# A two-model transformer step on one core: chosen mask ends the routing chain, second affine step beside the next index queries, residual factor inside the affine steps, MLP norm factor applied at the MLP's end

## The reference, cut to what matters

```
# first kind, l = 0, 1                                    ALPHA = 4 ** 0.25
mix = token_mixers(x, ...)               # differential and sparse attention, gates, w_out
x   = layer_norm(ALPHA * x + mix, ln1_g, ln1_b)
ffn = hierarchical_moe(x, ...)           # top group of 4, top 2 of its 8 experts, per token
ple = sigmoid(x @ w_ple_gate) * (p @ w_ple)
x   = layer_norm(ALPHA * x + ffn + ple, ln2_g, ln2_b)
# second kind, l = 0, 1
x = x + hybrid_mixer(rms_norm(x, attn_norm), ...)   # three attentions, gates, w_out
h = rms_norm(x, mlp_norm)
x = x + square(relu(h @ w_mlp_up)) @ w_mlp_down
# at the end
out = rms_norm(x, final_norm)
```

## Time and profile before

| what | value |
|---|---|
| three runs | 2030.92, 2035.6, 2040.48 us; median 2035.6 |
| the profiled execution | 2033.11 us, its span 2031.3 us |
| PE busy | 1913.3 us (94%) |
| DVE busy | 1414.3 us (70%) |
| ACT busy | 1076.6 us (53%) |
| POOL busy | 88.5 us (4%) |
| chain that ended last | 78% PE, 13% DVE, 4% ACT, 2% DMA, 1% POOL |

### The profile page before, as it was taken

One profiled execution on the slowest core, in us unless ns is written; L12 is line 12 of the kernel. 1 busy time (PEld: TensorE's weight loads), 2 busy tenths in 40 slices (PEclk: granted clock), 3 DMA queues, 4 the chain that ended last, 5 costly groups with the idle time before them and its releaser, 6 DMA issues.

```text
span 2031.3 us, 31158 instructions
## 1 busy us (share of the span) xinstructions
PE 1913.3 (94%) x12576; PEld 1750.0 (86%) x12576; DVE 1414.3 (70%) x2295; ACT 1076.6 (53%) x1686; POOL 88.5 (4%) x87
## 2 busy tenths in 40 slices
PE   7889989999889999999997899999998999999997
PEld 6779879999778898799896889998997889998997
DVE  5876778888668767898886666675445666675444
ACT  5454557777444545676773544444444645344443
POOL 2000010000010000100000000001001000001001
PEclk9999989999889999999998999999999999999999
DMA  7426169999444262799993343354554442454552
GB/s 288 145 84 235 48 261 408 389 408 420 167 166 146 104 229 71 296 414 374 422 421 121 130 154 137 125 187 148 190 191 170 157 160 105 146 184 148 187 189 82
DMA packets 60762, 426.77 MB, mean 210 GB/s; under 512 B 6928, under 2 KB 7056, under 8 KB 11584
## 3 DMA queue, kind: packets, MB, share of 16 engines
q1 hardware_dynamic: 59616, 421.65, 54.8%
q0 software_dynamic: 416, 1.81, 0.2%
q10 hardware_dynamic: 576, 1.19, 0.2%
HBM read 423.58 MB, written 1.05 MB: 209 GB/s over the span
## 4 chain that ended last, share of the span: by engine, by line
PE 78%; DVE 13%; ACT 4%; DMA 2%; issue 1%; POOL 1%; DVEq 0%; SPq 0%; ACTq 0%; POOLq 0%
PE bank L1041 63%; PE scp L1041 10%; DVE WSl L1384 4%; ACT WSh L1927 1%; PE bank L1135 1%; PE bank L1258 1%; ACT SC L1976 1%; DMA PT<-wts 1%; DMA ring<-wts 1%; PE bank L1120 1%; POOL sm L2163 1%; PE bank L1162 1%; DVE sm L1528 1%; DMA A<-wts 1%; PE bank L1278 1%
## 5 line engine op out<-in xcount | busy, mean ns | idle before, releaser
L1384 DVE TENSOR_TENSOR WSl<-ring,WSh 128x1024 fp32r<-128x1024 f32 (+3 forms) x512 | 591.2, 1198 | 213.9 <-ACT WSh L1927 212.2
L1927 ACT CAST WSh<-ring 128x1024 fp32r<-128x1024 f32 (+3 forms) x512 | 498.4, 1026 | 200.7 <-PE bank L1041 103.9
L1041 PE MATMUL bank<-XTh,WSh 128*128 128x256 f32 x1216 | 350.4, 288 | 7.2 <-DVE A L1563 4.4
L1041 PE MATMUL bank<-XTl,WSh 128*128 128x256 f32 x1216 | 346.6, 285 | 0.0
L1041 PE MATMUL bank<-XTh,WSl 128*128 128x256 f32 x1216 | 346.3, 285 | 0.0
L1041 PE MATMUL bank<-WSh,FA 128*128 128x512 f32 (+1 forms) x848 | 303.5, 391 | 3.9 <-DVE FA L1824 2.3
L1041 PE MATMUL bank<-WSl,FA 128*128 128x512 f32 (+1 forms) x680 | 264.0, 388 | 0.0
L1041 PEld LDWEIGHTS bank<-XTh,WSh 128*128 128x128 f32 x1216 | 236.1, 194 | 9.3 <-issue 5.5
L1041 PEld LDWEIGHTS bank<-XTl,WSh 128*128 128x128 f32 x1216 | 236.1, 194 | 0.2
L1041 PEld LDWEIGHTS bank<-XTh,WSl 128*128 128x128 f32 x1216 | 235.8, 194 | 0.0
L1041 PE MATMUL bank<-WSh,XTh 128*128 128x512 f32 (+4 forms) x544 | 205.3, 377 | 18.1 <-DVE WSl L1384 15.0
(11 more groups left out here) (279 smaller groups left out, 2939.4 us busy)
## 6 DMA issues: line engine op xcount, KB each, us to landing
ring<-wts SPq DMA_DIRECT2D x264, 1024.0 KB, 4.9
V<-wts SPq DMA_DIRECT2D x40, 1024.0 KB, 12.7
PT<-wts SPq DMA_DIRECT2D x30, 1024.0 KB, 9.7
H<-wts SPq DMA_DIRECT2D x28, 1024.0 KB, 9.3
GT<-wts SPq DMA_DIRECT2D x12, 1024.0 KB, 13.6
A<-wts SPq DMA_DIRECT2D x8, 1024.0 KB, 7.3
ring<-wts SPq DMA_DIRECT2D x8, 584.0 KB, 7.0
ring<-wts SPq DMA_DIRECT2D x4, 832.0 KB, 8.0
```

What stands on the lines that cost most here:

```text
L1041: return nc.tensor.matmul(dst, lhsT, rhs, start=start, stop=stop)
L1384: nc.vector.tensor_tensor(lo[:, c], buf[:, c], hi[:, c].bitcast(F32), ALU.subtract).then_inc(*lo_done.inc(("block", i)))
L1927: nc.scalar.copy(hi[:, c], buffers[s.buffer][:, c]).then_inc(*hi_done.inc(("half", i, k)))
```

## The change

1. `chosen` (MK) becomes a step of its own at the end of the routing chain, and the `lead` values become 14, 16 and 99, so that the chain ends ahead of the split that follows.
2. PE's spreading of the gains becomes the step `spread`, and DVE's part `affine` goes tile by tile. For `ln2` of the first layer, the two tiles stand after the index queries' steps of the second layer (`first_layer`, `if l:`).
3. ALPHA moves into the affine step: both instructions become scalar_tensor_tensor with the factor. POOL's multiplications go, except `scale_x` at `l == 0`.
4. `ROUTE_LATE` and `kept` stand after the eighth gather, not after the fourth.
5. In the second kind, `w_out`'s rows are transposed from X itself, the first half ahead of the last `w_out` block. `normed` "mlp" is gone. `factor` takes 1 / (mean square + eps), and `add_y` multiplies the MLP's result by it.
6. At the end, tile 0's statistics stand ahead of tile 1's sums, the final gain's row is spread into two banks ahead of the last block, and one instruction per half tile writes the output, which goes out in halves.
7. The pair of bn_stats after each `w_out` half stands behind both sums, in all four layers.
8. `pace` around the "ST" transposes is set otherwise; `spare` is empty there, and no instruction moves.

```diff
+    def affine(self, name, l, halves=range(T)):
+        for t in halves:
+            self.add("affine", name=name, l=l, t=t, scp=self.now("scp"))
...
                 f()
+            if l:
+                self.affine("ln2", l - 1, (c,))
...
-        self.add("scale_x", l=l)
+        if l == 0:
+            self.add("scale_x", l=l)
...
-        for c, self.lead in enumerate((0, 0, 12, 18, 18, 0)):
+        for c, self.lead in enumerate((0, 0, 14, 16, 99, 0)):
...
                 self.spare.extend(("route", dict(l=l, t=t, n=n)) for n in ROUTE_ORDER for t in range(T))
+                self.spare.append(("chosen", dict(l=l)))
...
-            if k == 3:
+            if k == KD - 1:
                 for n in ROUTE_LATE:
...
-        self.add("normed", name="mlp", l=l, n=D)
+        blocks = [f for c in range(2) for f in self.wide("w_out_2", "w_out", DEPTH + l, c, 512 * c, 512, ("merged", 2, l),
+                                                         owner="dve", row=l, fa=fa)]
         xt = self.use("XT", "pe")
-        self.turn_split("mlp", l, KD, xt=xt)
+        for f in blocks[0:3]:
+            f()
+        self.turn_split("mlp", l, 4, xt=xt)
+        blocks[3]()
+        self.turn_split("mlp", l, 4, at=2, xt=xt)
+        self.add("factor", l=l)
...
+                if l == DEPTH - 1 and q == 3 and j == 3:
+                    ends = [self.bank("dve") for _ in range(2)]
+                    self.add("final_row", l=l, u=ends)
...
-                    if s.name in ("ln1", "ln2", "attn", "mlp"):
+                    if s.name == "mlp":
+                        pe.wait_ge(dve_done, "x_out", DEPTH + l, s.j // 2)
+                    elif s.name in ("ln1", "ln2", "attn"):
...
+                if what == "mlp":
+                    nc.vector.scalar_tensor_tensor(x_, y, FACTOR[:, t, 1:2], x_, ALU.mult, ALU.add).then_inc(*dve_done.inc(*names))
...
                         nc.vector.scalar_tensor_tensor(xs, bank[u[t] % 4][:, :], 0.5, xs, ALU.mult, ALU.add).then_inc(
-                            *dve_done.inc(("bank", u[t])))
-                        dve.wait_ge(dve_done)
+                            *dve_done.inc(("bank", u[t]), ("x_out", l, s.c), ("x_out", l, s.c, t)))
+                    for t in range(T):
+                        xs = X[:, t, s.c * 512:(s.c + 1) * 512]
+                        dve.wait_ge(dve_done, "x_out", l, s.c, t)
                         nc.vector.bn_stats(MIX_STATS[:, t, s.c * 6:s.c * 6 + 6], xs).then_inc(*dve_done.inc())
...
+                    nc.vector.scalar_tensor_tensor(X[:, t, :], H[:, t, :], factor, g, ALU.mult, ALU.mult).then_inc(*dve_done.inc())
...
+                    nc.vector.scalar_tensor_tensor(X[:, t, :], b, factor, X[:, t, :], ALU.mult, ALU.add).then_inc(
+                        *dve_done.inc(("affine", s.name, l, t), *([("scp", s.scp)] if t else [])))
...
+                elif s.kind == "factor":
+                    for t in range(T):
+                        nc.vector.bn_aggr(FACTOR[:, t, :], MIX_STATS[:, t, 0:12]).then_inc(*dve_done.inc())
...
+                    nc.vector.reciprocal(f, f).then_inc(*dve_done.inc(("factor", l)))
...
-                elif s.kind == "embedded" and s.c == 0:
-                    pool.wait_ge(dve_done, "affine", "ln1", l, 1)
-                    nc.gpsimd.tensor_scalar(X[:, t, :], X[:, t, :], ALPHA, None, ALU.mult).then_inc(*pool_done.inc(("scaled", l, t)))
```

More of the change, by code:

```diff
@@ L358, in first_layer @@
         self.fill()
+        self.no_more_than(0)
+        self.pace = 1
         self.turn("DT", l, 16, P)
@@ L488, in first_layer @@
             self.turn_split("ln2", l, KD, xt=self.use("XT", "pe"))
-        self.add("affine", name="ln2", l=l, scp=self.use("scp", "dve"))
+        self.add("spread", name="ln2", l=l, scp=self.use("scp", "dve"))
+        if l == DEPTH - 1:
+            self.affine("ln2", l)
     def down(self, l, e):
@@ L1031, in sync_program @@
                 elif s.kind == "final":
-                    sp.wait_ge(dve_done, "out", 0)
-                    e.dma_start(out[0], H[:, 0, :]).then_inc(*out_done[0].inc(("all",)))
+                    for c in range(2):
+                        sp.wait_ge(dve_done, "out", 0, c)
+                        e.dma_start(out[0][:, 512 * c:512 * c + 512], H[:, 0, 512 * c:512 * c + 512]).then_inc(*out_done[0].inc(("all",)))
                     sp.wait_ge(out_done[0], "all")
@@ L1203, in tensor_program @@
                     last.then_inc(*pe_done.inc(("bank", u), *([("read", i), ("FA", s.fa)] if s.c == 3 else [])))
-                elif s.kind == "affine":
+                elif s.kind == "spread":
                     scp_free(s.scp)
@@ L2149, in scalar_program @@
                 elif s.kind == "final":
-                    act.wait_ge(dve_done, "out", 1)
-                    e.dma_start(out[1], H[:, 1, :]).then_inc(*out_done[1].inc(("all",)))
+                    for c in range(2):
+                        act.wait_ge(dve_done, "out", 1, c)
+                        e.dma_start(out[1][:, 512 * c:512 * c + 512], H[:, 1, 512 * c:512 * c + 512]).then_inc(*out_done[1].inc(("all",)))
                     act.wait_ge(out_done[1], "all")
@@ L2187, in gpsimd_program @@
                         power(1, base + 2 * t, (s.name, l, t))
+                elif s.kind == "final":
+                    for t in range(T):
+                        power(1, 64 + 2 * t, ("final", l, t))
                 elif s.kind == "clear":
```

106 lines of the change are left out of this document (56 added, 50 removed).

## The result

The changed kernel takes 2014.25 us (median of four runs, 2010.68 to 2016.85) against 2036.46 for the kernel before (four runs beside them): a ratio of 0.9888, 95% interval 0.9869 to 0.9907. The profiled execution has a span of 2014.2 us, 17.1 less than before. The forecast was 2017.0, faster.

What follows compares the result with a forecast made beforehand. TensorE, 78% of the chain that ended last, was taken to bound the kernel, with gains only at its pauses or lower clock. 5.4 + 11.2 + 1.6 - 1.3 + 1.6 = 18.5 us; 2035.6 - 18.5 = 2017, range 2009 to 2026.

Steps and rivals of the forecast that it cites:

- Second layer's start: Index queries of the second layer: TensorE's 4.51 us wait for VectorE's split goes and clock returns, net 5.4 us gained.
- Both causes: Second layer's late split: VectorE was in the affine step, then GpSimd's multiplication of X slowed the split's second half.
- the new wait: Second layer's start: TensorE waits 0.45 us for a split behind the affine tile now placed between the query blocks.
- Junctions: From w_out to the MLP, in two layers: the gap shrinks from 7.9 to 2.8 us; 11.2 us gained with clock.
- the rival by the clock: MLP behind the early transposes: TensorE goes on at 1.2 GHz, 36 us lost, 2053 us; chance 0.03.
- the clock's part in the last layer: Last layer's first MLP block: 0.9 us back from the shorter pause, possibly lost if transposes don't count as activity.
- the factor's multiplication: Additions at the MLP's end: applying the norm's factor there costs nothing, 0.69 us with or without a scalar.
- Routing: Routing into the experts, two layers: mask first loads H sooner, less the later small step's cost; 1.6 us gained.
- about 1.15 us: Second layer's routing: how much sooner H is loaded, since the next split's cast waits for its block to land.
- Statistics: First kind's w_out, two layers: statistics behind both sums make the norm wait 0.65 us longer each, -1.3 us.
- The end: Final norm and output: last store issued 1.4 us sooner and half a tile landing 0.2 faster; 1.6 us gained.
- rival (d): Slower: TensorE stays at 1.2 GHz behind the early transposes; both MLPs' first 192 matmuls lose 36 us, 2053; chance 0.03.

Runs made afterwards that it cites:

- e5: Kernel before with ALPHA in the affine instructions at their old place, so no GpSimd multiplication there: 2030.29 us against 2038.52, ratio 0.9964.
- e6: Kernel before with the affine tiles moved between the index query blocks, GpSimd's multiplication by ALPHA kept: 2031.88 us, ratio 0.9975.
- e2: Kernel before with only the w_out-to-MLP change (transposes from X in halves, factor in the additions): 2025.82 us against 2036.45, ratio 0.995.
- e3: Kernel before with only the mask made right behind the one-hot rows, small routing step unmoved: 2030.3 us against 2036.45, ratio 0.9971.
- e4: Kernel before with only the new end (early tile 0 statistics, four products, output in halves): 2032.45 us against 2036.45, ratio 0.9979.
- e9: Changed kernel with all sixteen MLP transposes behind w_out's last block, none early: 2013.39 us against 2036.33 for the kernel before, ratio 0.9892.
- e8: Changed kernel with ROUTE_LATE and kept back beside the fourth block's gather copies: 2010.82 us against 2038.52 for the kernel before, ratio 0.9891, two runs.
- e7: Changed kernel with each tile's first-kind statistics back right behind its own sum: 2012.9 us against 2038.52 for the kernel before, ratio 0.9902.
- e10: The changed kernel run again, nothing altered: 2011.94 us against 2036.33 for the kernel before, ratio 0.9886.
- e1: Kernel before with only the affine step's change (tiles moved, ALPHA in its instructions): 2031.07 us against 2036.45, ratio 0.998.
- e11: Changed kernel with both the statistics and the small routing step at their old places: 2009.23 us against 2036.33 for the kernel before, ratio 0.9863.
- e12: As e11, with both affine tiles behind the first two splits of 1,024 columns: 2011.86 us against 2036.33 for the kernel before, ratio 0.9881.

## Why the prediction was right

The sum was 18.5 us, low end 9.6, high end 23.4. The runs give 22.8 by the ratio, so the forecast was right in its mechanisms and 4 us too small, with the result near its high end. The measured median of 2014.25 is only 2.8 below the forecast, since the median of the kernel before came out 0.9 higher than the one that I started from and the ratio is not that of the medians. The terms, by the stretches:

**1. Second layer's start, 5.4: measured 5.6** between the prediction's own marks (19.20 to 13.56). Both causes were real (e5, e6), the new wait was 0.54 for the 0.45 of the walk through the queues, and the affine instructions take 1.22 us in their new form, as assumed. C by its medians gives 6.8, since the one profile that I read had a cheap pause: in the three others with the old code (e2, e3, e4) it was 4.8 to 5.4 us in place of 4.51. The 48 matmuls behind it took 8.5 to 9.0 us at a granted clock of 0.69 to 0.74, in place of 7.8 at 0.82. So the pause and the clock behind it were sized too small, and 20.4 us between the marks, not 19.20, is the usual length. The pause ends 18.6 to 19.1 us after the entry transposes in all four; why the clock rises sooner or later behind it, no run here tells.

**2. Junctions, 11.2: measured 12.1** (5.2 and 6.9). E and E' together take 581.1 to 581.7 us in the six profiles with the old code and 568.9 to 570.4 in the seven with the new. The gap of 2.8 us came out as 2.81. The last sum started 0.42 us after the last matmul, not late, and the granted clock was 1.00 in every window from 1365 to 1395, and from 1815 to 1845 in the last layer, so the rival by the clock never began, and the clock's part in the last layer was not lost to the early transposes. That layer's gap was 8.51 us, not 8.37, which makes 5.7, and its first MLP block gives 0.6 by the rows of the chain (23.93 to 23.33), where 0.9 was set; the rest of the 6.9 lies ahead of the junction, where the old code alone spreads by 1.3. The old block took 24.3 us in only four of its six profiles and 23.6 in the others, so this part of the term hung on the profile that was read. What the prediction didn't see is where the gain is from: the early half of the transposes is worth at most 0.25 us of each (e9), the norm's removal all the rest. It also put the factor's multiplication at nothing, and the rows that it names for that don't show it: at 2021.07 stands a bn_stats, no addition. Each of the four additions takes 0.73 to 0.75 us with a factor per token and 0.67 to 0.69 without, and the third layer's end is 0.26 us later for it (e2 has the same 162.84 us).

**3. Routing, 1.6: measured 2.6** (1.7 and 0.9). The first layer went by its steps: `H` 2.7 us sooner (2.6 forecast), 1.2 us taken by the small step (1.2 forecast). In the second the step that failed is "about 1.15 us" for `H` and "0.2" for the split: `H` came 2.35 us sooner behind the router's transposes than in the profile that I read (41.4 to 39.1 us). The landing of the block is at work as assumed: with the change the split behind the routing waits 0.5 us for its cast, and starts 28.5 us after the transposes. But before it started at 30.9 in the profile that I read, with the one-hot rows 1.0 us later than in the five others with the old code, where it is 29.8 to 30.0. Against these it gains 1.3 to 1.5 us, close to the 1.15. In three of the five the affine step then stood 1.1 to 1.3 us more for TensorE's spreading of the gains, which no profile with the change shows. The small step costs next to nothing there (e8). What reaches the second expert's next blocks is 0.9 us; in e3 the rest goes to the clock behind the pause.

**4. Statistics, -1.3: measured -0.9** (0.45 by e7's rows in the first layer, 0.48 by stretch D in the second). No time tells so little apart; this term rests on the rows and the stretch alone.

**5. The end, 1.6: measured 2.1.** The last store is issued 28.34 us after the start of the last MLP block, in place of 29.70: 1.36 sooner, as forecast (1.4). The part that was mis-sized is the landing: 2.5 us from issue to the span's end in place of 3.2, so 0.7 gained where 0.2 was set. The lists of DMA issues say the same, 2.1 us for 256 KB and 2.8 for 512.

The two profiled spans differ by 17.1 us and not by 22.7, since some of it went back by chance in code that the diff does not touch. One such place is the first layer's attention. Windows of the changed kernel:

```profile
150.00:155.00 5.00, 3.58 (x23) 3.16 (x22) 4.97 (x5) 1.65 (x4) 0.00 (x0) 0.82 0.78 290
155.00:160.00 5.00, 5.00 (x25) 5.00 (x25) 4.45 (x14) 4.08 (x17) 0.00 (x0) 0.50 0.22 92
```

And of the same kernel in e10, as in the kernel before:

```profile
155.00:160.00 5.00, 5.00 (x44) 5.00 (x43) 3.99 (x12) 4.34 (x17) 0.00 (x0) 1.00 0.14 59
```

That is 19 matmuls fewer in 5 us. The stretch from 49 to 233 takes 183.7 to 184.2 us in four of the fourteen profiles (before, e1, e5, e10) and 185.6 to 187.8 in the other ten, with either code. One pair of profiles would have given the edit 17 us; the ratio of several runs gives 22.8 and the stretches 21 to 23.

One number of the prediction is off and changes nothing: twice 192 matmuls at 0.10 us more are 38 us, not 36, in rival (d).

## What to carry to other kernels

Where a split or copy that TensorE waits for stands in an engine's queue behind work that is needed 100 us later, write the needed one first; then see what GpSimd does beside it, since a multiplication of 5.5 us made a VectorE instruction of 0.23 us take 3.7. A norm ahead of a product whose result is only scaled by rows can be taken out of the path and applied behind the product: that was worth over 5 us at each place, and overlapping the transposes as well at most 0.25. To judge edits of 1 to 5 us in a kernel of 2,000, compare stretches between marks across many profiles, and run the unchanged kernel again to learn what chance does in each. The same holds for a forecast: the pause of 4.51 us and the slow block of 23.93 that it was built on were one profile's.

## What was not expected of the hardware

A stretch of the same instructions at the same place runs at the full clock in one execution and at half of it in the next (155 to 160 above), or the clock rises sooner in one than in the other. Three places of that kind were seen: 150 to 160 (19 matmuls fewer in 5 us), the last matmuls ahead of the first scatter (11.2 to 13.9 us from the last 128x64 group to the scatter, at 0.70 to 0.52), and the start behind a pause (e11 and e12, 0.7 us; the old pause of the second layer, 7.8 to 9.0 us for 48 matmuls).

An earlier start behind a pause can be worth less than it looks: in e3 the second expert's first 16 matmuls began 2.4 us sooner after the router's transposes and took 1.2 us longer, at the lower clock almost throughout. That is half of the start paid back, not all. Why the clock rose during that block in the kernel before, and only behind it in e3, no run here tells.
